# Attention with the values held still: one output matmul for two heads, probabilities scaled before their transposes

## What is computed

```python
def block_attention(q, k, v, sink):            # context tokens; with sink for D
        s = jnp.einsum("bqhgd,bkhd->bhgqk", qi, k).astype(jnp.float32) * scale
        if sink is not None:
            p = jax.nn.softmax(jnp.concatenate([s, sc], axis=-1), axis=-1)[..., :-1]
        else:
            p = jax.nn.softmax(s, axis=-1)
        return jnp.einsum("bhgqk,bkhd->bqhgd", p.astype(v.dtype), v)

def window_attention(q, k, v, k_ctx, v_ctx, sink):   # latent tokens, mixer D
        s_loc = jnp.where(valid, s_loc, NEG_INF)
        p = jax.nn.softmax(jnp.concatenate([s_loc, s_ctx, sink_col], axis=-1), axis=-1)
        return (jnp.einsum("bhgqk,bkhd->bqhgd", p[..., :span], vw)
                + jnp.einsum("bhgqk,bkhd->bqhgd", p[..., span:-1], v_ctx))
```

## Time and profile before

| | us |
|---|---|
| median of 3 runs | 5593.83 (5588.25 to 5594.8) |
| the profiled execution, own time | 5605.9 |
| its span | 5604.1 |
| attention of layer 0, from its first query transpose to the first matmul of the merge | 373.0 to 636.9, 263.9 long; PE busy 251.3, DVE 144.1, ACT 96.7 |
| attention of layer 1, the same | 3156.2 to 3422.6, 266.4 long; PE busy 254.2, DVE 144.2, ACT 96.7 |
| one latent tile of it (412.1 to 469.4) | 57.3 |

### The profile page before, as it was taken

How to read it: one execution, slowest core, us unless ns; L and a number is a source line. 1 busy time by engine, 2 the same in 40 slices (tenths; PEclk the granted TensorE clock), 3 DMA queues, 4 the chain that set the end, 5 groups by cost and what they waited for, 6 DMA issues and landing times.

```text
span 5604.1 us, 47094 instructions
## 1 busy us (share of the span) xinstructions
PE 4472.4 (80%) x14736; PEld 2601.9 (46%) x14736; DVE 3694.6 (66%) x8129; ACT 887.5 (16%) x2536; POOL 1583.3 (28%) x1310
## 2 busy tenths in 40 slices
PE   6999996889797666666689999978887876666665
PEld 4866785444443222222258567754444432222222
DVE  1745316688687888876608453177886878888765
ACT  1023201111211111111111332101111111111111
POOL 0000000334334454455400000013443345444552
PEclk9999998999899888888899999989998998888887
DMA  6100142899989999999761002339998999999996
GB/s 267 45 31 1 63 150 110 328 377 369 358 353 358 421 422 421 421 420 422 330 240 38 31 1 79 139 125 361 376 378 347 351 373 421 422 421 421 419 422 282
DMA packets 226377, 1585.28 MB, mean 283 GB/s; under 512 B 26064, under 2 KB 28368, under 8 KB 46672
## 3 DMA queue, kind: packets, MB, share of 16 engines
q0 software_dynamic: 184320, 1342.26, 59.2%
q1 hardware_dynamic: 41808, 240.02, 11.3%
HBM read 1579.03 MB, written 3.15 MB: 282 GB/s over the span
## 4 chain that ended last, share of the span: by engine, by line
PE 40%; DMA 33%; DVE 17%; issue 3%; DVEq 3%; ACT 2%; POOL 1%; SPq 0%; POOLq 0%; ACTq 0%
DMA B<-tables,R 18%; PE ps L478 8%; DMA A<-tables,R 6%; PE ps L488 5%; PE ps L619 5%; DMA H<-tables,R 4%; DVE A L1469 4%; DVE B L1437 3%; DMA B<-ws 3%; PE ps L604 2%; PE ps L495 2%; PE ps L508 2%; PE ps L724 2%; DMA R<-tables,R 2%; DVE A L1437 2%
## 5 line engine op out<-in xcount | busy, mean ns | idle before, releaser
L478 PE MATMUL ps<-B,A 128*128 128x512 f32 x2048 | 1179.5, 723 | 555.1 <-ACT A L893 555.0
L446 POOL DMA_INDIRECT B<-tables,R x716 | 866.0, 1209 | 1860.2 <-PE ps L478 814.9
L1437 DVE SCALAR_TENSOR_TENSOR B<-B,M 128x1024 f32<-128x1024 f32 x716 | 866.8, 1224 | 290.3 <-DMA B<-tables,R 262.9
L478 PEld LDWEIGHTS ps<-B,A 128*128 128x128 f32 x2048 | 448.5, 229 | 1209.4 <-ACT A L893 677.1
L478 PE MATMUL ps<-A 128*128 128x512 f32 x992 | 530.6, 670 | 155.2 <-ACT A L893 155.1
L488 PE MATMUL ps<-H,B 128*128 128x384 f32 (+1 forms) x2048 | 595.0, 445 | 66.6 <-DMA B<-ws 44.0
L446 POOL DMA_INDIRECT A<-tables,R x356 | 440.0, 1236 | 582.5 <-PE ps L478 370.6
L488 PEld LDWEIGHTS ps<-H,B 128*128 128x128 f32 x2048 | 399.7, 196 | 264.5 <-issue 56.2
L1437 DVE SCALAR_TENSOR_TENSOR A<-A,M 128x1024 f32<-128x1024 f32 x356 | 433.5, 1225 | 128.7 <-DMA A<-tables,R 116.2
L887 ACT ACTIVATE T<-T 128x2 f32<-128x2 f32 (+1 forms) x448 | 91.6, 205 | 2351.3 <-DVEq L1439 2351.1
L478 PEld LDWEIGHTS ps<-A 128*128 128x128 f32 x992 | 208.0, 217 | 442.3 <-issue 230.9
(11 more groups left out here) (206 smaller groups left out, 5052.3 us busy)
## 6 DMA issues: line engine op xcount, KB each, us to landing
B<-ws SPq DMA_DIRECT2D x120, 1024.0 KB, 6.8
B<-ws SPq DMA_DIRECT2D x128, 768.0 KB, 7.9
B<-tables,R POOLq DMA_INDIRECT x716, 18.4
A<-tables,R POOLq DMA_INDIRECT x356, 14.8
R<-tabs SPq DMA_DIRECT2D x2, 2176.0 KB, 12.3
H<-tables,R POOLq DMA_INDIRECT x192, 16.9
x<-xin SPq DMA_DIRECT2D x1, 2560.0 KB, 9.3
y<-M SPq DMA_DIRECT2D x1, 2560.0 KB, 7.9
```

The lines of the kernel that those rows point to most:

```text
L446: pool.indirect_dma_start(out=ring[s], out_offset=None, in_=tables[:, :], in_offset=bass.IndirectOffsetOnAxis(ap=EI[:, n:n + 1], axis=0),) ...
L478: mm = pe.matmul(ps[:, bk + c, :], diag[PE_AT[n] % DIAGS], v_row[:, c * 512:(c + 1) * 512], start=(n % SLOTS == 0), stop=(PE_AT[n] + 1 == ...
L1437: v.scalar_tensor_tensor(out=u_row, in0=u_row, scalar=1.0, in1=h2[:, g.tile, :], op0=ALU.mult, op1=ALU.mult, accum_out=dots[:, o:o + 1])
```

## The change

The value product is turned round. The values (128 keys x 64 channels) are the stationary operand, and the transposed probabilities of two heads at a time, 256 columns, move. Even heads of a group of four go to PSUM partitions 0 to 63 and odd ones to 64 to 127, so the output has channels on the partitions. Hence `QO`, its transposes (L760) and its scaling (L1290) are gone, and a new `outputs` copies 256 columns for each group of four heads. Since queries now lie along the columns, the output can't be scaled by a number per partition; so VectorE scales the probabilities ahead of their transposes, in place (`inverse`). The value products of a group are issued together, after the transposes of the following group's first unit (positions 5, 9, 13), and the last group of a tile behind the query transposes of the next. The units are visited by `ORDER`, which alternates four windowed and four full ones. `keep_running` has 2 matmuls instead of 6 from the third tile on (`n` of 2 and more), and waits for an output copy.

```diff
+        PT = [A[:, 0:2560].rearrange("p (i c n) -> p i c n", i=5, c=4), M[:, 1280:3328].rearrange("p (i c n) -> p i c n", i=4, c=4)]
...
+                def values(n, t, g):
+
+                    u, at = ORDER[4 * g], 4 * n + g
+                    pt, nb, c = PT[windowed(u)], blocks(t, u), (u % HEADS) // GROUP * HD + windowed(u) * P
+                    pe.wait_ge(a_pa.sem, a_pa.at(l, n * UNITS + 4 * g + 4))
+                    pe.wait_ge(a_pd.sem, a_pd.at(l, n * UNITS + 4 * g + 4))
+                    pe.wait_ge(a_on.sem, a_on.at(l, at - 1))
+                    for i in range(nb):
+                        block = 0 if t is None else (1, 2, 3, 4, 6)[i] if not windowed(u) else t + i if i < 3 else 6
+                        for odd in range(2):
+                            last = pe.matmul(ps[odd * HD:odd * HD + HD, 6 + g % 2, 0:2 * P], V[:, block, c:c + HD],
+                                             pt[:, i, 2 * odd:2 * odd + 2, :], start=(i == 0), stop=(i == nb - 1))
+                    last.then_inc(a_o.sem, 1)
...
-                    keep_running(6)
+                    if n:
+                        values(n - 1, t - 1 if t else None, 3)
+                    keep_running(n, 6 if n < 2 else 2)
...
+                    def transposes(p):
+
+                        u = ORDER[p]
                         split = dve_blocks(t, u)
...
+                        pe.wait_ge(a_p.sem, a_p.at(l, u0 + p + 1))
+                        pe.wait_ge(a_pa.sem, a_pa.at(l, u0 + p))
+                        pe.wait_ge(a_pd.sem, a_pd.at(l, u0 + p))
+                        for i in range(blocks(t, u)):
+                            bank, o = (4, i) if i < split else (5, i - split)
+                            last = pe.transpose(ps[:, bank, o * P:(o + 1) * P], Pb[p % 2][:, i * P:(i + 1) * P], ident)
+                        last.then_inc(a_t.sem, 1)
+
+                    for p in range(UNITS + 1):
+                        if p < UNITS:
+                            scores(p)
+                        if p:
+                            transposes(p - 1)
+                        if p in (5, 9, 13):
+                            values(n, t, p // 4 - 1)
...
+                def outputs(n, g):
+
+                    u, o = ORDER[4 * g], PLACE[n]
+                    j = (u % HEADS) // 2
+                    act.wait_ge(a_o.sem, a_o.at(l, 4 * n + g + 1))
+                    act.copy(BRc[CHUNK[n]][:, 3 if windowed(u) else 2, j:j + 2, o:o + P],
+                             ps[:, 6 + g % 2, 0:2 * P].rearrange("p (j n) -> p j n", n=P)).then_inc(a_on.sem, 1)
...
+                    def inverse(p):
+                        u, e = ORDER[p], p % 2
+                        v.wait_ge(a_exp.sem, a_exp.at(l, u0 + p + 1))
+                        total = sm[:, 2, e:e + 1]
...
+                        v.reciprocal(sm[:, 4, e:e + 1], total)
                         v.drain()
...
+                        probs = Pb[e][:, 0:blocks(t, u) * P]
+                        v.tensor_scalar(out=probs, in0=probs, scalar1=sm[:, 4, e:e + 1], scalar2=None, op0=ALU.mult)\
+                            .then_inc(a_p.sem, 1)
...
+                    for p in range(UNITS + 1):
+                        if p:
+                            inverse(p - 1)
+                        if p < UNITS:
+                            maxima(p)
+                        if p:
+                            pt_copy(p - 1)
...
+ORDER = [0, 1, 2, 3, 8, 9, 10, 11, 4, 5, 6, 7, 12, 13, 14, 15]
+SIDE = [p % 2 * 2 + p % 4 // 2 for p in range(UNITS)]
```

More of the change, by code:

```diff
@@ L303, in program @@
         a_pd = sig("a_pd", UNITS * TILES, 1)
[L304 to L307 removed]
+        a_p = sig("a_p", UNITS * TILES)
+        a_o = sig("a_o", 4 * TILES)
+        a_on = sig("a_on", 4 * TILES, 2)
         rw_dg = sig("rw_dg", 8)
@@ L752, in attention @@
-                    for u in range(UNITS + 2):
-                        if u < UNITS:
-                            scores(u)
-                        if u:
-                            transposes_and_values(u - 1)
-                    pe.wait_ge(a_on.sem, a_on.at(l, u0 + UNITS))
-                    for i in range(8):
-                        last = pe.transpose(ps[:, 4 + i // 4, (i % 4) * P:(i % 4 + 1) * P], QO[:, i * P:(i + 1) * P], ident)
-                    last.then_inc(ot_ps.sem, 1)
+                        pe.wait_ge(a_p.sem, a_p.at(l, u0 + p + 1))
@@ L768, in _ @@
                     attention(t + 1, t)
+                values(TILES - 1, TILES - 2, 3)
                 def gate_rows(i):
@@ L1286, in pt_copy @@
                         v.drain()
-                    def out(u):
-                        v.wait_ge(a_o.sem, a_o.at(l, u0 + u + 1))
-                        v.tensor_scalar(out=QO[:, u * HD:(u + 1) * HD], in0=ps[:, 6 + u % 2, 0:HD],
-                                        scalar1=sm[:, 4, u % 2:u % 2 + 1], scalar2=None, op0=ALU.mult).then_inc(a_on.sem, 1)
-                    for u in range(UNITS + 2):
-                        if u < UNITS:
-                            maxima(u)
-                        else:
-                            v.drain()
-                        if 1 <= u <= UNITS:
-                            pt_copy(u - 1)
-                        if u >= 2:
-                            out(u - 2)
+                        probs = Pb[e][:, 0:blocks(t, u) * P]
```

127 lines of the change are left out of this document (42 added, 85 removed).

## The result

| | us |
|---|---|
| changed kernel, median of 4 runs | 5709.43 (5698.17 to 5732.89) |
| kernel before, median of 4 runs on the same chip | 5594.32 (5588.25 to 5595.99) |
| ratio | 1.0213, 95% interval 1.018 to 1.0247 |
| the profiled execution after, own time and span | 5706.25 and 5704.5 |

The kernel became 2.1% slower. The forecast was 5618 with a range of 5582 to 5662: the sign was right, the size was not, and the time lies outside the range.

The account below looks back on a forecast made before the run. PE bounds a unit now; after the change a softmax loop through VectorE and ScalarE would. Per layer 4 + 3 x 0.2 + 2.9 + 4 x 1.1 = 11.9 us, 24 for both, takes 5593.8 to 5618, range 5582 to 5662.

Parts of the forecast that it names:

- The loop: Each unit: sum, reciprocal, scaling, next maximum, exponential in series; 2.71 us for a full unit, 2.88 for a windowed one.
- The scaling: VectorE's multiplication of probabilities by the reciprocal: 0.56 us for 640 columns, 0.50 for 512, from a line through two traced widths.
- the maximum's rate: Rival of dearer scaling: 0.26 and 0.19 us more a unit, 29 in all, 5647; shares 0.15 with two other cases.
- The values in one piece: Value groups between transposes and scores, 0.11 us a pass: maximum late 1.27 at positions 5 and 13, 2.03 at 9.
- the 0.14 that the forecast left out: Pause of 0.14 us on the way into each value group, from a tiling mode change; 5 us in all, not summed.
- The seam: From a tile's last maximum to the next tile's first: 10.8 us against 14.8 before, 4.0 shorter.
- The context tile: Context tile of each layer: 4 us longer, 2.1 from its units and 2 from the full clock returning later.
- The last latent tile: Last latent tile of a layer, up to the merge: 2.9 us longer, 4.2 more less 1.3 saved at its end.
- The clock: Falls to half clock at every second of five seams between tiles: 1.1 us for each of four latent tiles.
- half clock within the tiles: Rival in latent tiles: 2 us more a unit, 43 if every sixth of 128 units, 5661; shares 0.15 with two others.
- three cases with 0.15 together: Slower rivals: scaling at the maximum's rate 5647, no overlap of column tiles 5676, half clock within the tiles 5661; together 0.15.
- 0.2 forecast for each: Each of the first three latent tiles: intervals 4.2 us longer, seam 4.0 shorter, so 0.2 longer before the clock term.

Follow-up runs that it names:

- the filler: The changed kernel plus one unread matmul of 256 columns a unit in the latent tiles, ahead of TensorE's wait for the scaled probabilities: 5626.56 us, ratio 1.0056.
- the pieces without a filler: The changed kernel with each group's value products issued in three pieces at three positions, outputs two positions later, no unread matmul added: 5776.73 us, ratio 1.029.
- the filler of 128 columns: The changed kernel plus one unread matmul of 128 columns a unit in the latent tiles, in place of 256: 5686.64 us, ratio 1.0163.
- the scaling alone: The kernel before, with VectorE scaling the probabilities ahead of their transposes and the value products left as they were: 5934.8 us, ratio 1.0603.

## Why the prediction was wrong in size

Point by point, by its own steps:

- **The loop.** Forecast 2.71 and 2.88 us a unit; 2.72 and 2.88 in the changed kernel where the clock is full. The sum's 446.03 + 0.19, the reciprocal behind it and the scaling at 0.55 and 0.49 (forecast 0.56 and 0.50) are as worked out. Right.
- **The scaling.** The line through the rows of 64 and 1024 columns held, not the maximum's rate. The Trainium skill, VectorE: DVE Perf Modes, Mode 2×_2P, has a tensor_scalar from SBUF use both read ports even for fp32. The trace agrees: 128 columns more cost 0.06 us in the scaling from SBUF (0.49 to 0.55) and 0.13 in the maximum from PSUM (0.69 to 0.82).
- **The values in one piece.** 0.11 a pass (453.41 to 455.71 for twenty). Positions 5 and 13 forecast 1.27 late, measured 4.09 - 2.71 = 1.38; position 9 forecast 4.91, measured 5.02. Right, a little low: the way into the group costs some 0.1 more than was put (452.82 to 453.41 is 0.59 for four transposes, where 0.45 was taken), and the 0.14 that the forecast left out belonged in the sum. By the Trainium skill, TensorEngine Tiling (Array Packing), Key Properties, a change of tiling mode drains TensorE; a pause of 0.14 us at such a place agrees with it.
- **The seam.** Forecast 10.8; 11.1 with the filler, so the chain was right, and 13.85 in the changed kernel, at half clock in part.
- **The context tile.** Forecast +4; from 373.44 to 410.03 it takes 36.6 against 32.1, +4.5. Right.
- **The last latent tile.** Forecast +2.9; +4.0 with the filler (62.6 against 58.6), a little low.
- **The clock.** Here is the step that failed: this term of the sum was put at 1.1 us a tile, 9 for both layers, and the runs show some 9.4 a tile, 75 for both layers. The forecast took a fall "at every second of the five seams" and left half clock within the tiles to a rival: "2 us a unit, 43 if it holds for every sixth of the 128 latent units", as one of three cases with 0.15 together. Measured: 27 to 31 us at half clock in each of the first three latent tiles of a layer and 35 in the last, which cost 6.8 to 11.3 us a tile and 83 in the median. The price of a unit was put too high (a windowed unit wholly at half clock takes 4.49, 1.6 more; a full one 0.76 more), and the number of units far too low: it is five intervals in a row from the third unit on, one to three near the end, and the seam. In tile 1 these are 5.1, 1.5 and 2.8 us (13.85 against the 11.07 of the filler's seam), 9.4 in all.

Why it happened: the forecast itself had "PE's busy share in the stage well below 95%", 2.2 of 2.71 us in a full unit. It worked out TensorE's place inside the loop at full clock only. But the earlier trace rows already had the clock falling behind a stretch in which PE was busy 2.07 of 3.40 us, and the change puts a pause into every unit. Once at half clock TensorE is the bound again, 3.5 to 4.5 us a unit against the loop's 2.7 to 2.9. The Trainium skill, TensorE: Matmul & The Clock Gate, A second HAM failure mode, describes such going back and forth between the two levels for a bf16 kernel in which TensorE idles for short times again and again between groups of matmuls; it puts no price on it. This fp32 trace shows the same, at 9.5 us in 68.5.

The terms other than the clock came out low by a little. The stage takes 278.6 us with the fillers in layer 0, 14.7 more than before, where the forecast without its clock term had 7.5 a layer; in layer 1 it takes 278.3, 11.9 more. Of the 7.2 us that layer 0 is over, the first three latent tiles are 5.5 (61.6, 59.0 and 58.6 against 58.5, 57.3 and 57.3, with 0.2 forecast for each), the last one 1.1 and the context tile 0.7. What part of this is the fillers' own work, no run separates.

What stays open is what exactly decides a fall. The runs show that the first fall of a tile has its cause near it, that it is gone in every tile with 256 columns a unit, and that with 128 it comes in four of eight tiles. They do not give a rule.

## What to carry to other kernels

When a change takes work off TensorE and leaves a loop through VectorE and ScalarE as the bound, its spared time becomes pauses, and pauses can cost the clock: work out the stage at half clock as well, and if TensorE is the bound there, that case is a likely one, not a tail. The test is cheap: put an unread matmul ahead of the wait. If the time falls and the granted clock rises with it, the clock was the cause, and the better cure is to cut the loop (here, transposes one unit later, maximum ahead of scaling), which made the same change a gain of 0.24% in place of a loss of 2.1%. And a schedule that spreads dense work evenly can be the worse one, if the dense piece was what brought the clock back; here that is the likely reading of the pieces without a filler, not a shown one.

## What was not expected of the hardware

- Added work made the kernel faster: 32 fillers a tile, counted in passes, took 83 us away.
- With the filler of 128 columns the same instructions at the same place took 69.1 us in layer 0 and 61.0 in layer 1 of one execution, at clocks of 0.82 and 0.96.
- The half clock can hold itself for a whole tile: with the scaling alone PE was busy 94.17 of 97.40 us at 0.55. Busy for nearly all of the time did not bring the full clock back there, while it did after 17.1 us in the changed kernel, where a group of sixteen passes of values had begun 2.3 us earlier (439.90).
